# A causal mask moved from TensorE products into a GpSimd select, and three weight blocks in other slots

## The reference, cut to what matters

```python
def fox_attend(q, fq, pq, k, v, fk, pk):
    s = jnp.einsum('bqhd,bkhd->bhqk', q, k).astype(jnp.float32) * (HEAD_DIM ** -0.5)
    s = s + jnp.swapaxes(fq, 1, 2)[..., :, None] - jnp.swapaxes(fk, 1, 2)[..., None, :]
    s = jnp.where(pq[:, None] >= pk[None, :], s, -jnp.inf)
    p = jax.nn.softmax(s, axis=-1)
    return jnp.einsum('bhqk,bkhd->bqhd', p.astype(v.dtype), v)
```

## Time and profile before

| | |
|---|---|
| median of 3 runs | 681.82 us (679.54 to 683.3) |
| span of the profiled execution | 678.7 us |
| PE busy | 656.1 us, 97% |
| VectorE, ACT, GpSimd busy | 385.9, 266.4, 144.4 us |
| share of PE in the chain that ended last | 86% |

### The profile page before, as it was taken

How to read it: one execution, slowest core, us unless ns; L and a number is a source line. 1 busy time by engine, 2 the same in 40 slices (tenths; PEclk the granted TensorE clock), 3 DMA queues, 4 the chain that set the end, 5 groups by cost and what they waited for, 6 DMA issues and landing times.

```text
span 678.7 us, 13245 instructions
## 1 busy us (share of the span) xinstructions
PE 656.1 (97%) x5183; PEld 564.7 (83%) x5183; DVE 385.9 (57%) x709; ACT 266.4 (39%) x486; POOL 144.4 (21%) x164
## 2 busy tenths in 40 slices
PE   6999999999999999999999998999999999999996
PEld 6989999898999889999999975776667755688884
DVE  5854916572455315149999766445443568554633
ACT  6636443111111245221213354645555666332321
POOL 3181112111111011223221140123222201121210
PEclk9999999999999999999999999999999999999998
DMA  7512103131100032345120364468666723113132
GB/s 208 172 43 63 32 2 76 39 87 32 33 8 27 5 85 71 93 133 155 32 62 1 106 178 147 119 177 256 178 205 187 221 108 109 48 62 125 63 125 93
DMA packets 59735, 67.29 MB, mean 99 GB/s; under 512 B 14156, under 2 KB 49883, under 8 KB 59673
## 3 DMA queue, kind: packets, MB, share of 16 engines
q1 hardware_dynamic: 54505, 51.37, 25.7%
q0 software_dynamic: 5168, 15.08, 7.5%
HBM read 57.71 MB, written 8.68 MB: 98 GB/s over the span
## 4 chain that ended last, share of the span: by engine, by line
PE 86%; DVE 7%; ACT 3%; issue 2%; DMA 1%; SPq 0%; DVEq 0%; ACTq 0%
PE PS L1925 14%; PE PS L1926 14%; PE PS L1927 14%; PE PS L1814 4%; PE PS L1815 4%; PE PS L1816 4%; PE PS L2214 4%; PE PS L2196 3%; PE PS L2171 3%; PE PS L2101 3%; PE PS L2149 3%; PE PS L2114 2%; DVE rows_odd L1693 1%; DVE YF L1572 1%; PE PS L2240 1%
## 5 line engine op out<-in xcount | busy, mean ns | idle before, releaser
L1925 PE MATMUL PS<-xh,wh 128*128 128x368 f32 x576 | 196.0, 340 | 0.3 <-DVE RA L1512 0.3
L1926 PE MATMUL PS<-xl,wh 128*128 128x368 f32 x576 | 190.2, 330 | 0.0
L1927 PE MATMUL PS<-xh,wl 128*128 128x368 f32 x576 | 189.7, 329 | 0.0
L649 POOL TENSOR_TENSOR wl<-wr,wh 128x1024 fp32r<-128x1024 f32 x23 | 59.7, 2597 | 263.1 <-ACT wh L1023 263.1
L1925 PEld LDWEIGHTS PS<-xh,wh 128*128 128x128 f32 x576 | 108.2, 188 | 4.1 <-issue 1.6
L1926 PEld LDWEIGHTS PS<-xl,wh 128*128 128x128 f32 x576 | 108.2, 188 | 0.9
L1927 PEld LDWEIGHTS PS<-xh,wl 128*128 128x128 f32 x576 | 108.2, 188 | 0.0
L1552 DVE RECIPROCAL RA<-RA 128x1104 f32<-128x1104 f32 x8 | 56.4, 7053 | 4.8 <-ACT RA L1169 4.6
L628 DVE TENSOR_TENSOR wr<-wr,small 128x1024 f32<-128x1024 f32 x24 | 35.9, 1495 | 35.3 <-DMA wr<-in_w_in_dram 35.2
L1814 PE MATMUL PS<-woh,yh 128*128 128x512 f32 x128 | 50.5, 395 | 0.0
L1816 PE MATMUL PS<-woh,yl 128*128 128x512 f32 x128 | 50.2, 392 | 0.0
(11 more groups left out here) (330 smaller groups left out, 1093.3 us busy)
## 6 DMA issues: line engine op xcount, KB each, us to landing
wr<-in_w_in_dram SPq DMA_DIRECT2D x24, 512.0 KB, 3.9
kpage<-in_cache_fox_k_dram SPq DMA_DIRECT2D x64, 192.0 KB, 3.0
RA<-in_cache_fox_v_dram POOLq DMA_DIRECT2D x32, 192.0 KB, 3.5
pagesB<-in_cache_fox_v_dram POOLq DMA_DIRECT2D x32, 192.0 KB, 3.7
YF<-in_x_prompt_dram SPq DMA_DIRECT2D x8, 512.0 KB, 7.0
xres<-in_x_prompt_dram SPq DMA_DIRECT2D x8, 512.0 KB, 3.7
out_y_p_dram<-zout SPq DMA_DIRECT2D x16, 256.0 KB, 2.1
wo_raw_a<-in_w_out_dram SPq DMA_DIRECT2D x6, 512.0 KB, 6.3
```

Of the source, the lines that this page charges most:

```text
L649: eng.tensor_tensor(low, wr[:, c % 2, :, 0:m], wh[:, c % 2, :, 0:m].bitcast(F32), ALU.subtract).then_inc(wlo_done, 1)
L1925: pe.matmul(out, high, xh[:, k, cols], start=(k == 0), stop=False)
L1926: pe.matmul(out, high, xl[:, k, cols], start=False, stop=False)
L1927: ins = pe.matmul(out, low, xh[:, k, cols], start=False, stop=(k == KT - 1))
```

## The change

GpSimd makes, for each tile's last chunk, a copy of minus F of both heads with -1e30 wherever the key lies behind the query (`affine_select`, function `mask_last`). VectorE's `row_max` reads this copy in the last chunk, and PE's mask products go, with the identity and mask that they used. The copies lie in two rooms in turn: for pair 0 in `nf_b`, which pair 1's rows fill later, and for pairs 1 and 2 in `RA`, where pair 0's rows were. So pair 1's rows are no longer loaded ahead of the walk, but after pair 0's last row maximum, as pair 2's are after pair 1's. A select for tile j + 2 is issued at tile j's "N". As the rooms in `RA` are in use until the last scores, output weight block 3 now lies over the sequences' probabilities, and blocks 4 and 5 over the rooms; ACT's copy of block 4 comes later.

```diff
+LAST = max(p1_chunks(j)[-1][1] - p1_chunks(j)[-1][0] for j in range(NTILE))
...
@@ -242,7 +245,7 @@
 SAMPLE, FIRST = ("proj", PROJ[0]), ("proj", PROJ[1])
-TAIL = {(2, 2, 0): [("W", 0), ("W", 1), ("W", 2)], (2, 2, 1): [("W", 3), ("W", 4)], (2, 2, 3): [("X", 0), ("X", 1)],
+TAIL = {(2, 2, 0): [("W", 0), ("W", 1), ("W", 2)], (2, 2, 1): [("W", 3)], (2, 2, 3): [("X", 0), ("X", 1), ("W", 4)],
         (2, 3, 1): [("X", 2), ("X", 3), ("W", 5), ("W", 6), ("Y", FIRST)], (2, 3, 3): [("X", 4), ("X", 5), ("W", 7)],
@@ -349,7 +350,7 @@
                                       ("wo_raw_b", [P, 2, D], F32))
-        wo_raw = [wo_raw_a[:, k, :] for k in range(6)] + [wo_raw_b[:, k, :] for k in range(2)]
+        wo_raw = [wo_raw_a[:, k, :] for k in (0, 1, 2, 5, 3, 4)] + [wo_raw_b[:, k, :] for k in range(2)]
         yh, yl = [yh0, yh1], [yl0, yl1]
@@ -549,6 +549,12 @@
+        def nf_last(p, j):
+
+            c0, c1 = p1_chunks(j)[-1]
+            room = RA[:, 3 * NT:3 * NT + 4 * LAST] if p else nf_b[:, :, :].rearrange("p i t -> p (i t)")[:, 0:4 * LAST]
+            return room.rearrange("p (u i t) -> p u i t", u=2, i=2)[:, EI[p, j] % 2, :, 0:c1 - c0]
+
         def exps_done(eng, p, j):
@@ -807,13 +813,11 @@
                 if k == 3:
-                    sp.wait_ge(p1_done, len(P1_UNITS))
-                elif k == 5:
                     drained(sp, ("s_attend", NB - 1))
+                elif k == 4:
+                    sp.wait_ge(p1_done, len(P1S))
                 elif k == 6:
                     s_ready(sp, ("T", 2, 2, 3))
-                elif k == 7:
-                    sp.wait_ge(p1_done, len(P1S))
                 sp.dma_start(wo_raw[k], wo_src[k]).then_inc(d_wo[k], 16)
@@ -861,9 +865,8 @@
             link(g.memset(one[:, :], 1.0))
-            for m in (ident, identb):
-                link(g.memset(m[:, :], 0.0))
-                keep(m[:, :], [[-1, P]], 0, 1, 1.0, ALU.not_equal, last=m is identb)
+            link(g.memset(ident[:, :], 0.0))
+            keep(ident[:, :], [[-1, P]], 0, 1, 1.0, ALU.not_equal, last=True)
@@ -908,8 +911,6 @@
             g.memset(pmax[:, :, :, :], -3e38).then_inc(pmax_low, 1)
-            link(g.memset(mask_neg[:, :], 0.0))
-            keep(mask_neg[:, :], [[-1, P]], 0, 1, NEG)
             link(g.memset(mask_new[:, :], 0.0))
@@ -938,7 +939,21 @@
                         load_values(0, i)
+            def mask_last(p, j):
+
+                n_, (c0, c1), q0 = EI[p, j], p1_chunks(j)[-1], NMETA + P * j
+                if j == 0:
+                    g.wait_ge(d_nfq if p else d_nfp, 32 * max(p, 1))
+                if n_ >= 2:
+                    p_, j_ = EXPS[n_ - 2]
+                    g.wait_ge(p1_done, P1S.index(("P1", p_, j_, len(p1_chunks(j_)) - 1)) + 1)
+                rows = (RA[:, 3 * NT:5 * NT].rearrange("p (i t) -> p i t", i=2) if p == 0 else nf_b)[:, :, c0:c1]
+                g.affine_select(out=nf_last(p, j), in_=rows, compare_op=ALU.is_ge, fill=NEG, base=q0 - c0,
+                                pattern=[[0, 2], [-1, c1 - c0]], channel_multiplier=1).then_inc(last_done, 1)
+
             g.wait_ge(in_full, NCHUNK)
+            for j in range(2):
+                mask_last(0, j)
             g.memset(sprob[:, :, :], 0.0).then_inc(sprob_zero, 1)
@@ -950,13 +965,18 @@
-            load_bias(1)
             for kind, key in PLAN:
                     load_values(*key)
-                elif kind == "N" and key == (1, NTILE - 1):
-                    g.wait_ge(p1_done, 2 * len(P1_UNITS))
-                    load_bias(2)
+                elif kind == "N":
+                    p, j = key
+                    if j == NTILE - 1 and p < 2:
+                        g.wait_ge(p1_done, (p + 1) * len(P1_UNITS))
+                        load_bias(p + 1)
+                        mask_last(p + 1, 0)
+                        mask_last(p + 1, 1)
+                    elif j < NTILE - 2:
+                        mask_last(p, j + 2)
             for n_, t in enumerate(PROJ[1:]):
@@ -1647,11 +1667,6 @@
                     dve.memset(VR[:, 9, :], 0.0).then_inc(meta_zero, 1)
-                    for out, full in ((ident_h, identb), (mask_neg_h, mask_neg)):
-                        for part in range(2):
-                            rows = slice(64 * part, 64 * part + 64)
-                            for to in range(2):
-                                dve.tensor_copy(out[64 * to:64 * to + 64, part, :], full[rows, :]).then_inc(halves_done, 1)
                 if c == 13:
@@ -1688,10 +1703,14 @@
                     dve.wait_ge(pmax_low, 1)
+                last = c + 1 == len(p1_chunks(j))
+                if last:
+                    dve.wait_ge(last_done, EI[p, j] + 1)
                 s_ready(dve, user)
                 for i in range(2):
+                    minus_f = nf_last(p, j)[:, i, :] if last else nf_rows[p][i][:, c0:c1]
                     ins = dve.tensor_tensor_reduce(score_rows(j, i)[:, c0:c1], s_head(user, i)[:, 0:c1 - c0],
-                                                   nf_rows[p][i][:, c0:c1], 1.0, -3e38, ALU.add, ALU.max,
+                                                   minus_f, 1.0, -3e38, ALU.add, ALU.max,
                                                    pmax[:, j, i, c:c + 1])
@@ -2155,27 +2174,19 @@
             chunk_stored(pe, NCHUNK - 2)
-            pe.wait_ge(halves_done, 8)
                 q0 = NMETA + P * j
-                d0 = max(c0, q0)
                 s_taken(pe, user)
                     ins = pe.matmul(s_head(user, i)[:, 0:c1 - c0], QK[rows, 3 + p, q0:q0 + P], QK[rows, p, c0:c1],
-                                    start=True, stop=(d0 >= c1))
-                if d0 < c1:
-                    for part in range(2):
-                        for i in range(2):
-                            rows = slice(64 * i, 64 * i + 64)
-                            ins = pe.matmul(s_head(user, i)[:, d0 - c0:c1 - c0], ident_h[rows, part, :],
-                                            mask_neg_h[rows, part, d0 - q0:c1 - q0], start=False, stop=(part == 1))
+                                    start=True, stop=True)
                 ins.then_inc(s_full, 1)
```

## The result

The changed kernel takes 689.35 us (median of 4 runs, 688.1 to 691.18) against 681.55 for the kernel before (4 runs, 679.54 to 683.3). The ratio is 1.0126, with a 95% interval of 1.0107 to 1.0146: slower by 7.8 us. The forecast was 689.8. The profiled execution's span is 687.6 us against 678.7, a difference of 8.9.

What follows compares the result with a forecast made beforehand. The prediction took PE, busy for 97% of the span, to bound the kernel. Its terms, +8.6 + 2.0 - 2.9 + 0 + 0.3 = +8.0 us, gave 689.8 us on the median, with a range of 684.5 to 695.5.

Steps and rivals of the forecast that it cites:

- Part 2: Pair 0, tile 2: VectorE, then PE, wait for a GpSimd select queued behind page loads; +8.6 us, from +5.3 to +9.5.
- The upper set: Slower select durations for tiles 0 to 2, from the one-input tensor_scalar: 0.49, 0.92 and 1.36 us; not the set taken.
- the rate of 1.8 to 2.6 cycles: GpSimd's cycles per element: tile 2's select some 1.2 to 1.7 us, up to 1.8 us more for all three.
- Part 3: After the stop in pair 0, TensorE's clock falls and must return; +2.0 us, from 0 to 4.
- Rival B: After the stop the clock stays low through pair 0; +32.3 us, 714 us; chance 0.05.
- Part 1: Attention stage: removed mask products give back 0.21 us in each of 14 units; -2.9 us, gain from 1.5 to 5.6.
- Part 4: Later selects in pair 0, at pair changes and in pairs 1 and 2 delay nothing; 0, at most 2 us.
- Part 5: End of the attention stage: ACT's later copy of an output weight block delays a turn; +0.3 us, 0 to 1.5.
- the stop's own lower bound of 5.3: Delay at pair 0's tile 2 if all nine transfers were issued back to back at 0.54 us each.
- Rival C: Rest of pair 0: PE's 2.9 us of waits vanish, partly giving the delay back; +5.1 us, 686.9; chance 0.07.
- D: Stop too short for the clock's fall, mask products worth their upper bound 5.6; +3.0 us, 684.8; chance 0.11.
- E: Attention stage paced by the loop from scores over row maximum to next scores; -6.4 us, 675.4, faster; chance 0.05.

Runs made afterwards that it cites:

- e1: Changed kernel with the selects of pair 0's tiles 2 and 3 moved ahead of GpSimd's memsets and page loads; 679.93 us, ratio 0.9998 to before.
- e5: Changed kernel with the selects of pair 0's tiles 2 and 3 behind three of the nine transfers; 681.95 us, ratio 1.0018 to before.
- e6: Changed kernel with the selects of pair 0's tiles 2 and 3 behind six of the nine transfers; 687.46 us, ratio 1.01 to before.
- e8: The changed kernel profiled and timed once more, nothing altered; 688.83 us, ratio 1.0122 to before.
- e2: Changed kernel with 60 filler products on PE in the stop, ahead of scores (0, 3, 1); 693.2 us, ratio 1.0191 to before.
- e3: Kernel before without the mask products, no select added, so diagonal blocks are not causal; 679.11 us, ratio 0.9983 to before.
- e7: Changed kernel with 33 filler products on PE in the stop, ahead of scores (0, 3, 1); 688.49 us, ratio 1.011 to before.
- e4: Kernel before with only the output weight blocks moved, with SP's waits and ACT's copy to match; one run, 684.22 us.

## Why the prediction was right, point by point

**Part 2, the stop: predicted 8.6, measured 7.7.** The mechanism is as told: VectorE released by the select, the select behind the ninth transfer, PE at the scores (0, 3, 1). The 0.9 too much is in the issues. I moved the old train (8.2 us from first page issue to the end of the small one) by the selects. Here the first four issues go back to back and not three, and the train is 399.70 to 407.07, 7.4 us. That GpSimd's order and nothing else makes the stop is shown by e1, e5 and e6.

The selects were slightly longer than predicted. Groups of GpSimd by form, from 396 to 600 (mean ns of one behind the bar's total):

```profile
L951 POOL TENSOR_SCALAR_AFFINE_SELECT RA<-nf_b 128x800 f32<-128x800 f32 x2 | 1.8, 878 | 0.0
...
L951 POOL TENSOR_SCALAR_AFFINE_SELECT RA<-nf_b 128x544 f32<-128x544 f32 x2 | 1.3, 638 | 0.0
...
L951 POOL TENSOR_SCALAR_AFFINE_SELECT RA<-nf_b 128x288 f32<-128x288 f32 x2 | 0.9, 428 | 13.0 <-DMA nf_b<-minus_Fp 13.0
```

428, 638 and 878 ns against 0.35, 0.59 and 0.82 us predicted: 0.88 ns an element ((878 - 428) / 512), and a fixed 0.17 us. The upper set, by the tensor_scalar row, is refuted. So is the rate of 1.8 to 2.6 cycles that I had quoted from the Trainium skill, GPSIMD Engine Reference, section 3.1. The same section gives 1.03 cycles for bodies of one or two operations; by estimate that is 0.86 ns at the 1.2 GHz it counts with. The trace agrees with this one, and it is the figure that I ought to have weighed.

**Part 3, the clock: predicted 2.0, measured 2.2.** It fell, and it came back after 5.6 us of work (409.12 to 414.7). The net lag grows by 2.07 or 2.08 us from the scores to tile 4 in all three executions in which PE stood for over 5 us (changed, e6, e8), and falls by 0.11 in all five others without mask products (e1, e2, e3, e5, e7). The difference is 2.18. e7 shows that it is the clock: same stop, same queue, same transfers, only PE kept busy. Rival B (low through pair 0) is dead. The Trainium skill, TensorE: Matmul & The Clock Gate, Part 1, has the slow clock as the default that activity releases; the fall in e6 and none in e7 agree. My reading of it, that an idle array pays each time it stops, was too wide: in e5 PE stood for 2.25 us and paid nothing.

The size came close partly by luck. I read the 20 instructions of the start as 20 filler products; they are ten, of two instructions each, as e2 showed. And the 0.14 us that I took for one at the full clock holds the drain of the last: e2 has 0.113 (13.56 us for 120). With it the same rows give 20 x 0.114 = 2.3 us. That the start is slow for the clock's sake is not shown either, since the windows have a granted clock of 1.00 there.

**Part 1, the products: predicted -2.9, measured -1.1.** This is the term that was mis-sized, above all by a factor of two in the price of a unit. I took 0.21 us from the start of the four to the next start, and did not look at what the next instruction would do without them. The kernel before has, ahead of and behind the four:

```profile
398.46 0.94 PE L2171 MATMUL PS<-YF 64*128 64x400 f32 x4
...
399.45 0.65 PE L2101 MATMUL PS<-ident,kpage 128*128 128x128 f32 x4
```

And the changed kernel:

```profile
398.39 0.94 PE L2188 MATMUL PS<-YF 64*128 64x400 f32 x4
399.27 0.66 PE L2120 MATMUL PS<-ident,kpage 128*128 128x128 f32 x4
```

From the scores to the transposes it was 0.99 us and is 0.88: 0.11 gained, not 0.21. The steps of the lag in e3 say the same. The first mask product could start 0.78 us behind the scores (399.24), the transposes directly behind the scores start at 0.88, so part of the 0.21 was a distance that is kept anyway. The count was off too: 14 units were to give it back, and it was 10 (1.09 / 0.11, with the 0.11 ahead of tile 4). From tile 4 to the end e3 gives 1.37 where the changed kernel gives 0.98. The lags of the single scores show where most of the 0.4 lies: between the scores of tile 5's first and second chunk, once in each pair, e3 gains a step of about 0.11 and the changed kernel none. There the weight load of the second chunk's scores waits for the row maximum of tile 4's last chunk. Pair 0, e3 and then the changed kernel:

```profile
412.02 0.49 DVE L1693 CUSTOM_DVE_ANT_0 rows_even<-PS,RA 128x320 f32<-128x320 f32 x1
412.98 0.30 PEld L2171 LDWEIGHTS PS<-YF 64*128 64x128 f32 x4 [0.67 <-DVE pmax L1693]
```

```profile
421.48 0.49 DVE L1712 CUSTOM_DVE_ANT_0 rows_even<-PS,nf_b 128x320 f32<-128x320 f32 x1 [0.17 <-PE PS L2188]
422.44 0.30 PEld L2188 LDWEIGHTS PS<-YF 64*128 64x128 f32 x4 [0.78 <-DVE pmax L1712]
```

From the start of that chunk's scores (411.16 and 420.51) to this row maximum pass 0.86 us in e3, 0.97 in the changed kernel and 0.96 before: the products are gone, and VectorE still begins as late as with them. It does so at the last chunks of tiles 2, 3 and 7 too (1.10, 0.86 and 0.99 us against 0.99, 0.75 and 0.88 in e3), though not at tile 6, nor at tile 0 of pairs 1 and 2 (1.10 and 0.70 in both). Why, no run separates: in the changed kernel it has one more semaphore to wait for there, and reads another copy of minus F. What the preparation of the mask was worth was rightly put at nothing: PE's first work starts at 3.75 us and not at 4.44, and by 15.6 us the lag is 0.01.

**Part 4, all other selects: predicted 0, measured 0.** Behind tile 4 the lag rises nowhere for good. At the change of pair GpSimd's and VectorE's timelines have, against the earlier trace rows:

```profile
449.92 1.03 POOL L951 TENSOR_SCALAR_AFFINE_SELECT RA<-nf_b 128x288 f32<-128x288 f32 x2 [6.51 <-DMA nf_b<-minus_Fp]
```

```profile
455.98 0.31 DVE L1712 CUSTOM_DVE_ANT_0 rows_even<-PS,RA 128x144 f32<-128x144 f32 x1 [0.15 <-PE PS L2188]
```

The selects end at 450.95 and are wanted at 455.98, released by PE. The trace names a select as what ended a wait of VectorE twice in the whole stage: the 9.30 us, and 2.13 at pair 0's tile 0, where it had waited 2.01 for mask products before. That is 0.13 of the 0.15 on entry, a term that I had not listed.

**Part 5, the weight blocks: predicted +0.3, measured 0.** ACT's copy costs PE 0.14 us once (0.38 against 0.24), and the next item takes it back.

**The sum.** 7.7 + 2.2 - 1.1 = 8.8, the net lag of 8.78; with 0.15 on entry it is the span's 8.9. (The 7.7 holds what the units ahead of the stop would have given back. Against e1, which has everything but the stop, the same lag is 8.0 + 2.2 - 1.4.) The forecast had +8.0. Its closeness owes something to luck: the stop was 0.9 and the blocks 0.3 too large, the clock 0.2 too small, and the products' gain 1.8 too large, which has the opposite sign in the sum. The medians differ by 7.8 us, closer still to 8.0, but they carry what falls outside the stage (last section); the lags do not. The ends of the range do not follow from its terms to the last digit either: +2.9 and +14.0 on 681.8 are 684.7 and 695.8, and the lower end does not use the stop's own lower bound of 5.3. Nothing hangs on that here. Rival C (the delay given back) does not hold: the lag is 9.91 from tile 4 to the last row maximum of pair 0, to a hundredth. D had the products at 5.6 and E a loop worth 15; e3 gives 1.7 for all of them.

No version here that keeps the whole computation beats the kernel before by more than the runs can tell; the best of them, e1_early, is equal to it. (e3, at 0.9983 [0.9968, 0.9998], leaves the mask out.)

## What to carry to other kernels

A small operation given to an idle engine costs not its duration but its place in that engine's list: look at what stands ahead of it, DMA issues included, and at who is waiting behind. Here moving two selects ahead of nine transfers was worth 10.2 us by the net lags (8.78 and -1.43), and 8.0 by the medians, each taken against before in its own comparison (+7.8 and -0.15). A stop of TensorE that is long enough (5.1 us here, but not 2.25) has a second price in the clock afterwards, which fillers that end before the wait does can remove. And the worth of an instruction that is taken out is read over the whole group, from its predecessor's start to its successor's, not from its own.

## What the runs showed of the hardware that I had not expected

**The clock falls in full work too.** In e3 the windows around 164 us, in the projection stage:

```profile
162.00:164.00 2.00, 2.00 (x33) 1.84 (x33) 0.99 (x5) 0.00 (x0) 0.00 (x0) 1.00 0.58 175
164.00:168.00 4.00, 4.00 (x37) 3.50 (x37) 1.12 (x3) 0.00 (x0) 0.00 (x0) 0.57 0.00 0
168.00:170.00 2.00, 2.00 (x12) 1.80 (x12) 0.86 (x4) 0.00 (x0) 0.00 (x0) 1.00 0.00 0
```

PE is busy throughout, ahead of the fall and in it. Of ten profiles six have such a stretch of 3.4 us between 162 and 169 us (e2, e3, e5, e6, e7, e8), e4 one of 6.8 us at 238 to 244, e8 a second one at 12 to 15, and before, changed and e1 none. By the starts of the projection's products (L1925 before), each stretch of 3.4 us near 165 adds 1.5 us to the lag and e4's adds 3.1. What starts it is not known.

**The other part of the spread is there by 23 us.** The same products lag there by -1.16 us (e2) to +0.83 (e4), where the windows show no low clock yet, and by 1.80 in e8, where they show one; from there the lag stays the same to 0.02 us up to the next stretch of low clock. What makes it I have not followed. Both parts show in the timed runs: of 23 runs of before in one comparison, the thirteen shortest have spans of 677.6 to 678.7 at mean clocks of 0.997 to 0.999. Of the ten others, 679.3 to 681.6, six have clocks of 0.994 or 0.995, and four have 0.996 or 0.997. Lags by stage are free of both, and medians of a few runs are not.

**A low clock that fell longer costs no more.** It was low for 6.8 us in e6 and for 10.2 in the changed kernel, and both lost 2.07 us: from the scores to the clock's return were 6.0 and 5.6 us, and the rest lay in time in which PE stood.

**Page issues.** From GpSimd, the first three or four are issued 0.55 us apart (2.19 us for four), and from then on mostly one per 1.15 us (0.54, and 0.6 of standing). How many go through at once is the same in each order of GpSimd's list: four in all profiles in which the first four follow the two memsets and the selects of tiles 0 and 1 (changed, e2, e6, e7, e8), three in before, e3, e4 and e1. Why, no run shows.
